# Weight sums of an encoder step, formed in DRAM: four 4 MB halves at once, or four groups of 512 columns spread over the program

## The chip, the cores and the metric

One Trainium2 chip, one NeuronCore, one execution of the whole program. The metric is the device time in microseconds (us). Kernel before: 3052.26 us, the median of three runs (3049.77 to 3056.08).

## The reference, cut to what matters

The program is one inference step of a hybrid encoder layer over 2048 prompt rows and 32 sample rows of width 1024. Three head groups (stick-breaking attention A, chunk-band softmax attention B, a gated recurrence C) work on one input projection; then come an output projection and a squared-ReLU MLP:

```
h = x + mixed @ w_o                          # 1024 x 1024
u = relu(rmsnorm(h, norm_ffn) @ w_up)        # 1024 x 4096
y = h + (u * u) @ w_down                     # 4096 x 1024
```

The product with `w_up` is done as a 2 x 2 block product with 7 multiplications in place of 8. Four of its seven weight factors are sums of the quadrants of `w_up`, each 512 rows x 2048 columns of float32, 4 MB. With w11 the top left quadrant, w21 the top right, w12 the bottom left and w22 the bottom right (the names of the changed code), they are:

```
sums[0] = w21 + w22      sums[1] = w11 + sums[0]
sums[2] = w11 + w21      sums[3] = w12 + sums[1]
```

They lie in `scratch_sums` in DRAM. GpSimd's DMA queue makes them: plain copies of a quadrant into its place, then DMAs that add another quadrant (or an earlier sum) to what lies there.

## The kernel before, in words

The program has three stages, one after the other: `front` (to about 329 us of the profile), `middle` (to about 1426 us) and `merge_and_ffn`, the last.

**The middle** runs four pieces of work as generators, interleaved by `plan`, a list of 846 letters. Each engine goes through that list on its own: at each letter it issues what the named piece has for that turn. B (96 turns, plan steps 0 to 168) is the chunk-band attention, A (196 turns, steps 160 to 572) the stick-breaking attention, C (169 turns, steps 565 to 845) the recurrence, and D (385 turns) a dense projection whose matmuls lie between the turns of the others. A DMA placed "at step k" on GpSimd is issued when GpSimd's own stream gets there, so it can run ahead of the other engines wherever GpSimd has nothing to wait for. SyncE (SP) issues every other DMA of the program, in one order: loads of keys, values and queries (L920 to L935), reloads of x (L564), stores of projected columns (L572, L577), loads of the recurrence (L1369 to L1389).

The sums are made by GpSimd beside that work. `begin_sums` at step 8 issues the four 4 MB copies (L1769); `add_halves` at step 282 waits for them and issues two adding DMAs (L1774); `add_third` at step 423 (L1778) and `add_fourth` at step 564 (L1782) issue one each, each after a wait for what it adds to. GpSimd waits for the last at the end of the middle. Its other work there: the mask of attention A (L976), scaling of a gated output (L590), the mask table (L1738 to L1759) and parts of C.

**The last stage** runs over three thirds of the rows (6 + 6 + 5 tiles of 128 rows and one of 32), `t` = 0, 1, 2. A third begins with the output projection, tile by tile (L2643); in it GpSimd turns each tile's sum of squares into a scale (L2140, L2143), 17 times in the whole stage. Then come 16 steps `p` of 256 hidden columns. `up(t, p, z)` (L2682) does the seven products z; `down(t, p)` (L2715) multiplies by `w_down` and adds into six accumulators through VectorE (L2481). The chunks of z = 6, 7, 5 and 3 come from `scratch_sums`, columns 128p to 128p + 127; those of 1, 2 and 4 from `w_up`. Each is 256 KB in 512 rows of 512 bytes, loaded by SP (L2028) into one of four staging buffers `stu`, rounded by ScalarE into one of seven buffers `uw..h` (L2166), the rest formed by VectorE in `uw..l` (L2350). VectorE's `uw..l` frees the staging buffer, and SP's next load waits for it. A step also loads 1 MB of `w_down` (L2038, one buffer `std`; split at L2180 and L2356). SP issues all this in one order; a load that waits holds back all behind it.

Of the kernel before, what the change touches and what calls it, by code (L numbers as in the profile page):

```python
# [15 lines left out]
ALU = mybir.AluOpType  # L16
# [1612 lines left out]
def middle(nc, ring, w_o, xhi, xlo, xt, w_in, lower_bounds, onorm, proj, tr, sources_a, sources_b, bias, sources_c, states, mix,  # L1629
           w_up, sums, used):  # L1630
# [4 lines left out]
    with ctx:  # L1635
# [16 lines left out]
        sum_begun, sum_added = S.sem("md_sum_begun"), S.sem("md_sum_added")  # L1652
# [83 lines left out]
        def _(pool):  # L1736
# [28 lines left out]
            copied, added = half_sums(w_up, sums)  # L1765

            def begin_sums():
                for out, half in copied:
                    nc.gpsimd.dma_start(out, half).then_inc(sum_begun, 16)  # L1769

            def add_halves():
                pool.wait_ge(sum_begun, 64)
                for out, half in added[0:2]:
                    nc.gpsimd.dma_start(out, half, accum_op=ALU.add, max_dma_last_dim=8192).then_inc(sum_added, 16)  # L1774

            def add_third():
                pool.wait_ge(sum_added, 32)
                nc.gpsimd.dma_start(added[2][0], added[2][1], accum_op=ALU.add, max_dma_last_dim=8192).then_inc(sum_added, 16)  # L1778

            def add_fourth():  # L1780
                pool.wait_ge(sum_added, 48)
                nc.gpsimd.dma_start(added[3][0], added[3][1], accum_op=ALU.add, max_dma_last_dim=8192).then_inc(sum_added, 16)  # L1782

            beside = {masks_at: make_masks, 8: begin_sums}
            for k, do in enumerate((add_halves, add_third, add_fourth)):
                beside[len(plan) * (2 + k) // 6] = do
            run(Dn.gpsimd(pool), B.gpsimd(pool), A.gpsimd(pool), C.gpsimd(pool), beside)
            pool.wait_ge(sum_added, 64)
# [17 lines left out]
def half_sums(w_up, sums):  # L1806


    half, rows = DFF // 2, D // 2
    top, low = slice(0, rows), slice(rows, D)  # L1810
    one, two = slice(0, half), slice(half, DFF)
    first = [(sums[0], w_up[top, two]), (sums[1], w_up[top, one]), (sums[2], w_up[top, one]), (sums[3], w_up[low, one])]
    added = [(sums[0], w_up[low, two]), (sums[2], w_up[top, two]), (sums[1], sums[0]), (sums[3], sums[1])]
    return first, added


def merge_and_ffn(nc, raw_at, nat_at, wo, nat2, mix, x, w_o, norm_ffn, w_up, w_down, sums, y):
# [16 lines left out]
    with ctx:  # L1834
# [297 lines left out]
        def _(pool):  # L2132
# [5 lines left out]
            for n, r in enumerate(r for th in FT for _, r in th):  # L2138
                pool.wait_ge(s["squared"], n + 1)
                nc.gpsimd.tensor_scalar(rstd[0:r, n:n + 1], ss[0:r, n:n + 1], 1.0 / D, EPS,  # L2140
                                        ALU.mult, ALU.add).then_inc(s["mean_ready"], 1)
                pool.wait_ge(s["mean_ready"], n + 1)
                nc.gpsimd.tensor_tensor(rstd[0:r, n:n + 1], rstd[0:r, n:n + 1], mhalf[0:r, 0:1],  # L2143
                                        ALU.pow).then_inc(s["rstd_ready"], 1)
# [599 lines left out]
def build(nc, a, outs):  # L2744
# [35 lines left out]
    kept = Map(nc, nc.sbuf_base, "")  # L2780
    with ExitStack() as ctx:
# [11 lines left out]
               (a["state_c"][0, 0], [csp[0, 0], css[0, 0]]), mix, a["w_up"][0], sums, used)  # L2793
# [26 lines left out]
```

## Time and profile before

| | |
|---|---|
| Runs (median of three) | 3052.26 us |
| The profiled execution | 3049.58 us |
| Its span, first to last instruction | 3047.8 us |
| TensorE matmul busy | 94% of the span |
| VectorE, ScalarE, GpSimd busy | 61%, 39%, 11% |
| TensorE's mean granted clock | 0.977 of 2.4 GHz |
| GpSimd's DMA queue | 33.55 MB, 8 DMAs of 4 MB |

The profile is of one execution, all times in us from its span's start. "Idle" of an engine is time in which it ran no instruction; the releaser named after it is what ended the last wait. The granted clock has two levels here, 2.4 GHz (1.0) and 1.2 GHz (0.5). DMA share is the mean busy share of the 16 DMA engines; q0 is GpSimd's DMA queue, q1 that of SP. A DMA's time "to landing" runs from its issue to its completion.

### The profile page before, as it was taken

How to read it: one execution, taken by the hardware profiler on the slowest of the kernel's cores; microseconds unless marked ns; L12 is line 12 of the kernel's file. 1: busy time of each engine (PE TensorE's matmuls, PEld its weight loads, DVE VectorE, ACT ScalarE, POOL GpSimd, SP SyncE). 2: the span in 40 equal slices, each digit the busy share in tenths (PEclk: the TensorE clock that was granted, in tenths of full speed). 3: DMA queues.
4: the chain of work that ended last, by engine and by line, in shares of the span. 5: the costliest groups of instructions: out<-in, count | busy, mean ns of one | idle time of the engine just before them, and what ended most of it. 6: DMA issues, size and time to landing. Idle time of an engine off the chain costs nothing.

```text
span 3047.8 us, 46651 instructions
## 1 busy us (share of the span) xinstructions
PE 2858.7 (94%) x17560; PEld 2502.4 (82%) x17560; DVE 1861.4 (61%) x2988; ACT 1182.1 (39%) x2448; POOL 336.9 (11%) x512
## 2 busy tenths in 40 slices
PE   7999589996998979987999999999999999999998
PEld 5788478885887879976888898988898988788887
DVE  5554244464655646786576666657666666587776
ACT  3331156543554523323343343334343433254442
POOL 2222110011000114563000000000000000000000
PEclk9999799998998989999999999999999999999999
DMA  8733642249333374452133232252332322444342
GB/s 263 250 126 121 235 144 80 80 127 232 95 101 97 94 204 136 133 184 100 60 116 92 83 104 87 91 193 72 91 104 87 104 86 96 151 118 135 114 128 96
DMA packets 412433, 381.90 MB, mean 125 GB/s; under 512 B 58124, under 2 KB 361838, under 8 KB 408114
## 3 DMA queue, kind: packets, MB, share of 16 engines
q1 hardware_dynamic: 407986, 345.37, 36.4%
q0 software_dynamic: 4224, 33.55, 4.3%
q8 instruction: 141, 2.31, 0.3%
q14 instruction: 82, 0.67, 0.1%
HBM read 310.81 MB, written 101.33 MB: 135 GB/s over the span
## 4 chain that ended last, share of the span: by engine, by line
PE 48%; DVE 2%; ACT 1%; issue 1%; DMA 1%; POOL 0%; POOLq 0%; DVEq 0%; ACTq 0%; SPq 0%
PE mf_psO L2715 23%; PE mf_psT L2682 18%; PE mf_psO L2643 5%; PE mf_psT L2617 1%; PE mf_psO L2682 1%; PE mf_psO L2701 0%; DMA mf_stu<-scratch_sums 0%; DVE mf_acc L2481 0%; DVE mf_hs L2432 0%; DVE mf_acc L2420 0%; DVE mf_dwl L2356 0%; ACT mf_psO L2222 0%; DMA mf_std<-in_w_down 0%; DVE mf_ow L2343 0%; DVE mf_uw2l L2350 0%
## 5 line engine op out<-in xcount | busy, mean ns | idle before, releaser
L2715 PE MATMUL mf_psO<-mf_dwh,mf_u 128*128 128x512 f32 x1920 | 613.2, 396 | 3.1 <-DVE mf_acc L2481 2.5
L2481 DVE TENSOR_TENSOR mf_acc<-mf_psO,mf_acc 128x1024 f32<-128x1024 f32 x256 | 313.2, 1223 | 279.7 <-PE mf_psO L2715 279.7
L2715 PEld LDWEIGHTS mf_psO<-mf_dwh,mf_u 128*128 128x128 f32 x1920 | 360.0, 188 | 101.6 <-issue 13.2
L2715 PE MATMUL mf_psO<-mf_dwl,mf_u 128*128 128x512 f32 x960 | 379.2, 395 | 0.0
L2180 ACT ACTIVATE mf_dwh<-mf_std 128x512 fp32r<-128x512 f32 x180 | 103.1, 624 | 518.3 <-PE mf_psO L2715 513.6
L2715 PEld LDWEIGHTS mf_psO<-mf_dwl,mf_u 128*128 128x128 f32 x960 | 180.0, 188 | 41.6
L994 ACT ACTIVATE md_wT<-md_psW 128x512 f32<-128x512 f32 (+4 forms) x232 | 128.5, 554 | 195.5 <-PE md_psW L1251 195.1
L438 PE MATMUL pj_psO<-pj_whi,xhi 128*128 128x512 f32 (+1 forms) x408 | 164.0, 402 | 0.4 <-DVE pj_wlo L359 0.4
L1070 DVE TENSOR_TENSOR_SCAN md_cp<-md_Aub,md_cp 128x512 f32<-128x512 f32 (+1 forms) x100 | 130.3, 1309 | 55.1 <-ACT md_Aub L1008 54.5
L438 PE MATMUL pj_psO<-pj_wlo,xhi 128*128 128x512 f32 (+1 forms) x408 | 162.4, 398 | 0.0
L438 PE MATMUL pj_psO<-pj_whi,xlo 128*128 128x512 f32 (+1 forms) x408 | 162.2, 398 | 0.0
L698 PE MATMUL md_psD<-wlo,xhi 128*128 128x256 f32 (+1 forms) x544 | 159.2, 293 | 0.0
L698 PE MATMUL md_psD<-whi,xlo 128*128 128x256 f32 (+1 forms) x544 | 159.0, 292 | 0.0
L698 PE MATMUL md_psD<-whi,xhi 128*128 128x256 f32 (+1 forms) x544 | 158.7, 292 | 0.0
L695 PE MATMUL md_psD<-xhi,whi 128*128 128x384 f32 (+1 forms) x384 | 136.8, 356 | 8.9 <-DVE wlo L636 8.9
L2140 POOL TENSOR_SCALAR mf_rstd<-mf_ss 128x1 f32<-128x1 f32 (+1 forms) x17 | 5.2, 305 | 1221.5 <-ACT mf_psO L2222 1221.5
L1175 PE MATMUL md_psZ<-md_KT,md_qhi 128*128 128x512 f32 (+5 forms) x288 | 99.9, 347 | 35.8 <-ACT md_Aub L1008 28.1
L2356 DVE TENSOR_TENSOR mf_dwl<-mf_std,mf_dwh 128x512 fp32r<-128x512 f32 x180 | 115.7, 685 | 20.7 <-ACT mf_dwh L2180 19.9
L695 PE MATMUL md_psD<-xlo,whi 128*128 128x384 f32 (+1 forms) x384 | 127.2, 331 | 0.0
L695 PE MATMUL md_psD<-xhi,wlo 128*128 128x384 f32 (+1 forms) x384 | 126.9, 331 | 0.0
L2457 DVE TENSOR_TENSOR mf_hs<-mf_hs 128x384 f32<-128x384 f32 (+1 forms) x186 | 95.6, 514 | 28.9 <-ACT mf_hs L2245 28.6
L2245 ACT ACTIVATE mf_hs<-mf_hs 128x384 f32<-128x384 f32 (+1 forms) x138 | 68.2, 494 | 111.3 <-DVE mf_hs L2449 85.9
(344 smaller groups left out, 7241.3 us busy)
## 6 DMA issues: line engine op xcount, KB each, us to landing
mf_std<-in_w_down SPq DMA_DIRECT2D x48, 1024.0 KB, 5.2
mf_stu<-scratch_sums SPq DMA_DIRECT2D x192, 256.0 KB, 2.9
mf_stu<-in_w_up SPq DMA_DIRECT2D x144, 256.0 KB, 3.6
wst<-in_w_in SPq DMA_DIRECT2D x24, 1024.0 KB, 5.3
scratch_sums<-in_w_up POOLq DMA_DIRECT2D x6, 4096.0 KB, 39.1
pj_wst<-in_w_in SPq DMA_DIRECT2D x36, 512.0 KB, 5.9
scratch_proj<-pj_ob SPq DMA_DIRECT2D x48, 256.0 KB, 2.0
pj_xin<-in_x_prompt SPq DMA_DIRECT2D x16, 512.0 KB, 7.3
```

Of the source, the lines that this page charges most:

```text
L438: last = nc.tensor.matmul(psO[n % NO][0:r, :], xa[:, k, c], wa[m % 2][:, k, :], start=k == 0 and j == 0, stop=k == KD - 1 and j == 2)
L695: last = nc.tensor.matmul(psD[n % NB][:, 0:r], wa[q % 2][:, k, e * P:(e + 1) * P], xa[:, k, cols], start=m == 0, stop=m == 23)
L698: last = nc.tensor.matmul(psD[n % NB][0:r, 0:256], xa[:, k, cols], wa[q % 2][:, k, :], start=m == 0, stop=m == 23)
L994: last = nc.scalar.activation(wT[j % 4][:, 0:full, 0:r], psW[j % WB][:, 0:full, 0:r], ACT.Copy)
L1070: nc.vector.tensor_tensor_scan(out=cp[i % NW][0:r, 0:w][:, ::-1], data0=u[0:r, 0:w][:, ::-1], data1=u[0:r, 0:w][:, ::-1], initial=init_v, ...
L1175: last = nc.tensor.matmul(psZ[i % ZB][0:r, x0:x1], qq[q][:, h, 0:r], KT[:, h, c0 + x0:c0 + x1], start=first, stop=not first)
L2180: nc.scalar.activation(d_buf(p)[0][:, cols], std[:, cols], ACT.Copy).then_inc(s["whi_d"], 1)
L2356: nc.vector.tensor_tensor(lo[:, cols], std[:, cols], hi[:, cols].bitcast(F32), ALU.subtract).then_inc(s["wlo_d"], 1)
L2481: nc.vector.tensor_tensor(acc[0:r, pos, :], psO[k % 2][0:r, :], acc[0:r, pos, :], ALU.add).then_inc(s["o_out"], 1)
L2643: last = nc.tensor.matmul(psO[k % 2][0:r, cols], xs[xa], ow[q][wa][:, w0:w0 + 512], start=at == 0 and j == 0 and e == 0, stop=at == 3 and ...
L2682: last = nc.tensor.matmul(out, wa[:, kk, :], xa[:, kk, 0:HB[t]], start=not again and kk == 0 and q == 0, stop=kk == KH - 1 and q == 2, ski ...
L2715: last = nc.tensor.matmul(psO[k % 2][0:r, cols], u[:, f, ua, c:c + P], wa[:, w0:w0 + 512], start=j == 0 and q == 0, stop=j == 1 and q == 2)
```

## The change

The eight DMAs of 4 MB become 32 of 1 MB: each half is cut into four groups of 512 columns. A group is eight DMAs: four copies, the first and second add after all four copies, the third add after those two, the fourth after the third. Rows of a DMA are now 2048 bytes long instead of 8192; each DMA still has 512 rows.

- Group 0 is made in the middle, one DMA at each of steps 200, 240, 280 and 320 (copies) and 370, 420, 470 and 520 (adds).
- Groups 1, 2 and 3 are made in the last stage by GpSimd, straight after the scales of the first third's six tiles: four copies in a row, then the adds with their waits, then the next group.
- SP waits, before each load of a chunk from `scratch_sums` in the first third, until the group that holds its columns is complete: p = 0 to 3 lie in group 0, 4 to 7 in group 1, 8 to 11 in group 2, 12 to 15 in group 3.
- GpSimd's wait at the end of the middle for the last add goes away.

```diff
-            beside = {masks_at: make_masks, 8: begin_sums}
-            for k, do in enumerate((add_halves, add_third, add_fourth)):
-                beside[len(plan) * (2 + k) // 6] = do
+            steps = {200: lambda: halves.copy(0, 0), 240: lambda: halves.copy(0, 1), 280: lambda: halves.copy(0, 2),
+                     320: lambda: halves.copy(0, 3), 370: lambda: halves.add_first(pool, 0),
+                     420: lambda: halves.add_second(pool, 0), 470: lambda: halves.add_third(pool, 0),
+                     520: lambda: halves.add_fourth(pool, 0)}
+            beside = {masks_at: make_masks, **steps}
             run(Dn.gpsimd(pool), B.gpsimd(pool), A.gpsimd(pool), C.gpsimd(pool), beside)
-            pool.wait_ge(sum_added, 64)
...
+class HalfSums:
+    GROUPS = 4
...
+        self.cols = DFF // 2 // self.GROUPS
...
+    def copy(self, g, i):
+        half = (self.w21, self.w11, self.w11, self.w12)[i]
+        self.nc.gpsimd.dma_start(self.of(self.sums[i], g), self.of(half, g)).then_inc(self.begun, 16)
+
+    def add(self, g, i, half):
+        self.nc.gpsimd.dma_start(self.of(self.sums[i], g), self.of(half, g), accum_op=ALU.add, max_dma_last_dim=8192
+                                 ).then_inc(self.added, 16)
+
+    def add_first(self, pool, g):
+        pool.wait_ge(self.begun, 64 * (g + 1))
+        self.add(g, 0, self.w22)
+
+    def add_second(self, pool, g):
+        pool.wait_ge(self.begun, 64 * (g + 1))
+        self.add(g, 2, self.w21)
+
+    def add_third(self, pool, g):
+        pool.wait_ge(self.added, 64 * g + 32)
+        self.add(g, 1, self.sums[0])
+
+    def add_fourth(self, pool, g):
+        pool.wait_ge(self.added, 64 * g + 48)
+        self.add(g, 3, self.sums[1])
...
@@ load_u, on SP
+                p, z = up_order[pos]
+                if t == 0 and z in (5, 6, 7, 3):
+                    sp.wait_ge(halves.added, 64 * (p * P // halves.cols + 1))
                 sp.dma_start(stu[:, c % NST, :].rearrange("p (k n) -> p k n", k=KH), chunk_src(*up_order[pos])
...
@@ GpSimd in the last stage, after the scales of third t
+                if t == 0:
+                    for g in range(1, halves.GROUPS):
+                        for i in range(4):
+                            halves.copy(g, i)
+                        halves.add_first(pool, g)
+                        halves.add_second(pool, g)
+                        halves.add_third(pool, g)
+                        halves.add_fourth(pool, g)
```

## Rows read from the trace of the kernel before

**Rows 1.** The page: busy tenths of TensorE in 40 equal slices, and its DMA share
```profile
PE   7999589996998979987999999999999999999998
DMA  8733642249333374452133232252332322444342
```

**Rows 2.** TensorE's waits from 326 to 1420 us: total, times, longest
```profile
PE md_psT L1200 <- DVE md_khl L1094: 45.6, 4, 25.0
PE md_psZ L1175 <- ACT md_Aub L1008: 28.1, 1, 28.1
PE md_psZ L1578 <- DMA md_rcg<-scratch_proj: 17.1, 1, 17.1
...
PE md_psZ L1187 <- DVE md_bt L1053: 8.2, 1, 8.2
```

**Rows 3.** DMA issues by line, whole program: count, KB each, median us to landing
```profile
mf_stu<-scratch_sums SPq DMA_DIRECT2D x192, 256.0 KB, 2.9
...
md_rcg<-scratch_proj SPq DMA_DIRECT2D x16, 256.0 KB, 5.2
```

**Rows 4.** Stretches with sums under way: each engine's busy us, PEclk, DMA share, GB/s
```profile
335.00:390.00 55.00, 18.93 (x90) 15.90 (x89) 7.35 (x14) 5.22 (x10) 0.00 (x0) 0.72 1.00 335
712.00:757.00 45.00, 19.44 (x171) 17.03 (x169) 11.98 (x16) 7.52 (x16) 4.59 (x7) 0.76 1.04 224
900.00:924.00 24.00, 10.30 (x78) 9.19 (x74) 4.57 (x6) 4.84 (x9) 0.65 (x1) 0.76 1.02 215
1093.00:1115.00 22.00, 9.61 (x86) 9.10 (x86) 3.35 (x6) 3.83 (x8) 0.99 (x2) 0.82 1.05 221
```

**Rows 5.** DMA queues, 376 to 385 us (copies under way): packets, MB, engines' share
```profile
q0 software_dynamic: 350, 2.77, 92.6%
q1 hardware_dynamic: 350, 0.12, 5.2%
```

**Rows 6.** DMA queues, 715 to 750 us (two adds under way)
```profile
q0 software_dynamic: 878, 7.06, 96.9%
q1 hardware_dynamic: 832, 0.43, 6.1%
```

**Rows 7.** SP's issues, 695 to 800 and 1099 to 1113 us: start, duration
```profile
714.41 38.81 SPq L577 DMA_DIRECT2D scratch_proj<-md_ob  x1
...
1100.61 4.93 SPq L577 DMA_DIRECT2D scratch_proj<-md_ob  x1
1105.70 5.00 SPq L1388 DMA_DIRECT2D md_rcv<-scratch_proj  x1
1110.75 2.60 SPq L1389 DMA_DIRECT2D md_rcg<-scratch_proj  x1
```

**Rows 8.** Half-clock stretches 346:370, 383.5:397, 735:766, 912.6:929.7, 1107:1124, their sum
```profile
sum 102.60, PE 27.02 PEld 23.52 DVE 14.47 ACT 7.54 POOL 7.05; mean PE 5.40 PEld 4.70 DVE 2.89 ACT 1.51 POOL 1.41
```

**Rows 9.** GpSimd in order of time, near 402 and near 1512 us
```profile
402.49 0.58 POOL L953 TENSOR_SCALAR_AFFINE_SELECT md_negm<-md_negm 128x1 f32<-128x1 f32 x2
...
1511.77 0.55 POOL L2143 TENSOR_TENSOR mf_rstd<-mf_rstd,mf_mhalf 128x1 f32<-128x1 f32 x1
```

**Rows 10.** DMA queues, 1636 to 1667 us (one step p)
```profile
q1 hardware_dynamic: 3968, 2.88, 31.8%
```

**Rows 11.** SP and ScalarE in order of time, last stage, chunk loads and splits
```profile
1581.11 3.17 SPq L2028 DMA_DIRECT2D mf_stu<-scratch_sums  x2
...
1598.46 0.36 SPq L2028 DMA_DIRECT2D mf_stu<-scratch_sums  x1
...
1548.15 0.63 ACT L2166 ACTIVATE mf_uw4h<-mf_stu 128x512 fp32r<-128x512 f32 x1 [2.22 <-DMA mf_stu<-scratch_sums]
...
1605.97 0.62 ACT L2166 ACTIVATE mf_uw4h<-mf_stu 128x512 fp32r<-128x512 f32 x1
```

**Rows 12.** The chain that ended last: two pieces, one step p
```profile
1604.98 16.80 PE mf_psO L2715 x72
1621.78 14.56 PE mf_psT L2682 x84
```

More of the change, by code:

```diff
@@ L1629, in middle @@
 def middle(nc, ring, w_o, xhi, xlo, xt, w_in, lower_bounds, onorm, proj, tr, sources_a, sources_b, bias, sources_c, states, mix,
-           w_up, sums, used):
+           halves, used):
     ctx = ExitStack()
@@ L1651, in middle @@
         maskstep = S.sem("md_maskstep")
-        sum_begun, sum_added = S.sem("md_sum_begun"), S.sem("md_sum_added")
         Dn = dense(nc, sems, mp, ring, xhi, xlo, xt, w_in, lower_bounds, onorm, psD, proj, tr)
@@ L1763, in make_masks @@
                 assert step == MASKSTEPS
[L1765 to L1782, printed above, removed]
-            beside = {masks_at: make_masks, 8: begin_sums}
-            for k, do in enumerate((add_halves, add_third, add_fourth)):
-                beside[len(plan) * (2 + k) // 6] = do
+            steps = {200: lambda: halves.copy(0, 0), 240: lambda: halves.copy(0, 1), 280: lambda: halves.copy(0, 2),
[3 more added lines that the diff above has]
+            beside = {masks_at: make_masks, **steps}
             run(Dn.gpsimd(pool), B.gpsimd(pool), A.gpsimd(pool), C.gpsimd(pool), beside)
-            pool.wait_ge(sum_added, 64)
         @block.scalar
@@ L1803, in middle, with __init__, of, merge_and_ffn @@
     return nat_at, wo, nat
[L1806 to L1817, printed above, removed]
+class HalfSums:
+    GROUPS = 4
+    def __init__(self, nc, w_up, sums, begun, added):
+        self.nc, self.begun, self.added = nc, begun, added
+        self.cols = DFF // 2 // self.GROUPS
+        half, rows = DFF // 2, D // 2
+        top, low = w_up[0:rows, :], w_up[rows:D, :]
+        self.w11, self.w21 = top[:, 0:half], top[:, half:DFF]
+        self.w12, self.w22 = low[:, 0:half], low[:, half:DFF]
+        self.sums = sums
+    def of(self, w, g):
+        return w[:, g * self.cols:(g + 1) * self.cols]
+    def copy(self, g, i):
[16 more added lines that the diff above has]
+        self.add(g, 3, self.sums[1])
+def merge_and_ffn(nc, raw_at, nat_at, wo, nat2, mix, x, w_o, norm_ffn, w_up, w_down, sums, halves, y):
     NP = DFF // (2 * P)
@@ L2137, in _ @@
                                     base=0, pattern=[[-1, P]], channel_multiplier=1).then_inc(s["init"], 1)
[L2138 to L2144, printed above, removed]
+            n = 0
+            for t in range(NTH):
+                for _, r in FT[t]:
+                    pool.wait_ge(s["squared"], n + 1)
+                    nc.gpsimd.tensor_scalar(rstd[0:r, n:n + 1], ss[0:r, n:n + 1], 1.0 / D, EPS,
+                                            ALU.mult, ALU.add).then_inc(s["mean_ready"], 1)
+                    pool.wait_ge(s["mean_ready"], n + 1)
+                    nc.gpsimd.tensor_tensor(rstd[0:r, n:n + 1], rstd[0:r, n:n + 1], mhalf[0:r, 0:1],
+                                            ALU.pow).then_inc(s["rstd_ready"], 1)
+                    n += 1
+                if t == 0:
[6 more added lines that the diff above has]
+                        halves.add_fourth(pool, g)
         @block.scalar
@@ L2780, in build @@
     kept = Map(nc, nc.sbuf_base, "")
+    halves = HalfSums(nc, a["w_up"][0], sums, nc.alloc_semaphore("sum_begun"), nc.alloc_semaphore("sum_added"))
     with ExitStack() as ctx:
@@ L2792, in build @@
                (lambda t0, r: proj[IC, t0:t0 + r, :], lambda t0, r: proj[GC, t0:t0 + r, :]),
-               (a["state_c"][0, 0], [csp[0, 0], css[0, 0]]), mix, a["w_up"][0], sums, used)
-    merge_and_ffn(nc, kept.base, nat_at, wo, nat, mix, x, a["w_o"][0], a["norm_ffn"][0], a["w_up"][0], a["w_down"][0], sums, y)
+               (a["state_c"][0, 0], [csp[0, 0], css[0, 0]]), mix, halves, used)
+    merge_and_ffn(nc, kept.base, nat_at, wo, nat, mix, x, a["w_o"][0], a["norm_ffn"][0], a["w_up"][0], a["w_down"][0], sums, halves, y)
 _INS = ["x_prompt", "x_sample", "cache_a_k", "cache_a_v", "cache_b_k", "cache_b_v", "state_c", "norm_mix", "w_in",
```

## Prediction

> **What bounds the kernel now.** I read the page's slices first: TensorE is at nine tenths nearly everywhere, and the lowest slices of the middle (5 at 305 to 381 us, 6 at 686 to 762) lie where the DMA row is high (6 and 9) [rows 1]. Then TensorE's waits in the middle [rows 2]: four kinds hold 99 us. By their time they are 25.0, 2.8 and 8.2 us between 341 and 389, 28.1 from 731, 14.5 from 910 and 17.1 from 1103 (the row of 45.6 holds 25.0, 2.8, 14.5 and one of 3.3 at 595, near no sum). That is 95.7 us.
>
> Next the stretches in which the eight 4 MB DMAs run: all DMA engines are busy (share 1.00 to 1.05) while TensorE works 18.9 of 55, 19.4 of 45, 10.3 of 24 and 9.6 of 22 us [rows 4]. The queue counts say why. With copies under way q0 and q1 each finish 350 packets, with adds 878 and 832 [rows 5, 6]: the DMA engines take one packet of each queue in turn. One of q0 is 8 KB and takes 0.926 x 9 us x 16 / 350 = 0.38 us (copy) or 0.969 x 35 x 16 / 878 = 0.62 us (add). Those of SP are small, so SP gets 5% or 6% of the time, and its small stores and loads pile up: an issue is stuck 38.8 us, others 4.9 and 5.0 [rows 7]. So at four places TensorE is bound by SP's starved queue, and everywhere else in the middle by its own work. In the last stage it is the chain without a gap, 16.80 + 14.56 = 31.36 us a step [rows 12].
>
> **1. The bursts leave the middle: -101 us.** The waits of 95.7 us go, but for what would stand there anyway. At 341 the loads that were waited for stand in SP's queue behind the four bias loads (4 x 128 x 640 floats, 1.3 MB), about 4 us at the rate of this stretch (335 GB/s [rows 4]): I leave 3. At 1103 the load waited for was issued at 1110.75 after two stuck issues of 4.93 and 5.00 us [rows 7]; without those it is issued near 1101.5, and 5.2 us of landing [rows 3] leave 5 of the 17.1. So 95.7 - 8 = 88 us. The idle engine also falls to half clock at these places: in five stretches of 102.6 us it is busy 27.0 us at 0.50 [rows 8], which at full clock is 13.5. Sum 101. Bounds: 80 (a fifth of the stalls turns out to be latency of the attention stages) and 109 (nothing remains). The reason against a smaller number is that every one of the four long waits starts 7 to 19 us after the burst does, and ends with it.
>
> **2. Group 0 in the middle: +1 us.** Eight DMAs of 1 MB. Step 200 comes before the first masked unit of A, so GpSimd passes it as soon as it is through A's opening (402.49 [rows 9]): the first copy runs in B, not in A. The others lie over A, the adds about 70 us apart. A copy puts 32 packets on each DMA engine. A packet of 2048 bytes is not in the trace; in proportion to size it is 0.38 / 4 = 0.095 us (copy) and 0.62 / 4 = 0.155 (add), and it can't be more than 0.38 and 0.62. I take the proportional value, since the packets' time is that of their bytes at the fabric's rate: 2.77 MB of copies in 8.3 us is 332 GB/s. So an add holds SP's queue for 32 x 0.155 = 5.0 us, a copy 3.0. The third add, a burst of 24 us, stalled TensorE for 14.5 [rows 2, 4]: 9.5 us of a burst are covered by loads made ahead. 5.0 is less. Bounds 0 and 4 x 3.0 + 4 x 5.0 = 32, all uncovered. GpSimd's own issues and waits are hidden: each DMA it waits for was issued 50 steps, some 70 us, before. What is queued behind such a wait are A's masks, which the chain needs; they are late only if an add takes over 60 us.
>
> **3. Groups 1 to 3 beside the last stage: +10 us.** They begin when GpSimd has done the sixth scale, 1511.77 + 0.55 [rows 9]. Engine time of a group: 128 packets x 0.095 + 128 x 0.155 = 32 us on each DMA engine; three make 96 us. SP's queue wants 31.8% of 31 us, 9.9 us a step, in 3968 / 16 = 248 packets of 0.040 us [rows 10]. A group then takes about 32 / (1 - 0.32) + three hand-overs of 2 to 3 us between add and add = 55 us, three 165, to about 1677. In a step's 31.4 us some 22 are free, so on the whole there is room; what costs is lateness of single loads.
>
> A chunk load is 32 packets on each engine. Beside adds it takes 32 x (0.155 + 0.040) = 6.2 us where it took 1.3: 5 us later, and a second and third behind it more, until the pair of adds is through (64 packets, 12.5 us). Beside copies it is 3 us later. Who has that much room? In a regular step the load issued at 1598.46 is used by ScalarE at 1605.97, and it lands in 2.9 us: 4.6 us of room [rows 3, 11]; VectorE comes to the result a little later still, which I put at 3 us more. At the start of the third there is none: ScalarE stands idle 2.22 us for the load that it uses at 1548.15 [rows 11]. VectorE takes these splits between its adds into the accumulators, which free TensorE's two output buffers, so a late chunk stops `down` as well. I take 2 us for the loads of 1526 to 1536 and 6 for those of 1545 to 1556, where the first and third adds of group 1 fall, and 0.5 for each of the four steps that follow: 8 + 2 = 10. Bounds: 0, and 3 x 16 = 48 (each group's adds, 4 x 5 us less 4 of room, in full).
>
> SP's new waits: for p = 0 to 3 they are met long before. The first one that could hold is that of p = 4, whose first summed chunk SP loads at 1581.11 [rows 11]. Group 1 is complete near 1512.3 + 55 = 1567, 14 us before; group 2 near 1622 for a wait at 1707, group 3 near 1677 for 1832. Cost 0; each us over 68 for group 1 would stop SP, and behind it the loads of `w_down` too. GpSimd's scales for the second third are due near 2080, long after. The wait removed at the end of the middle had been met since about 1115: 0.
>
> **Sum.** -101 + 1 + 10 = -90, against the profiled execution's 3049.6: 2959.6. The median of the runs stands 2.7 above that execution, so 2962.
>
> **Rivals.** *The late groups cost more (chance 0.18).* If packets of 2 KB are dearer than a quarter, or the queue's turn is longer, SP waits longer per packet. The rows show one packet for one, at 8 KB.
> The Trainium skill (DMA: Bandwidth & Descriptors, SWDGE vs HWDGE vs iDMA) says that an engine changes queue only at packet borders and that GpSimd's packets may hold several descriptors, preferably up to 4096 bytes. By that rule two rows of 2 KB could go in one turn, where the 8 KB rows of before could not show it; the trace agrees with the change of queue at each packet, and is silent on the pairing.
> Worked out from rows, two add packets in a turn make a chunk load 32 x (0.31 + 0.04) = 11.2 us, 10 later than now instead of 5; the 4.6 + 3 us of room are then passed in regular steps too, by 3 to 6 us in each of five steps, and the start costs 15 to 20: 35 to 50 in all. Time 2952 + 45 = 2997.
>
> *The stalls are only partly the bursts' (0.11).* TensorE then meets VectorE's or ScalarE's limits where it used to wait. For it: VectorE works 12.0 us of the 19.4 that TensorE works beside two adds, so it is not idle where TensorE runs [rows 4]. Against it: the slices between the bursts are at nine tenths [rows 1]. The lower bound above and 10 more: gain 60, time 2992.
>
> *The other side: a packet costs the same whatever its size (0.05).* The place is SP's wait at p = 4. With 0.38 and 0.62 us for 2 KB, a group takes 128 x 0.42 + 128 x 0.66 + 8 = 146 us. SP stops for 146 - 68 = 78 us, and at p = 8 and 12 until the third group is there: 3 x 146 - 320 = 118 us in all, more than the 101 gained. With 10 for contention: 3052 - 101 + 118 + 10 = 3079. It decides from 137 us a group (3 x 137 - 320 = 91). *That the change doesn't do what it says* holds for the first copy alone and costs nothing.
>
> **How the numbers follow.** Forecast 2962, chance 0.62, own range 2948 to 2978 (gain 109 less 5 to gain 80 less 6). The first two rivals reach to 3005, where the bounds 80 and 48 + 8 leave a gain of 24 at worst: the range 2946 to 3008 leaves out the third rival and the tails. A measurement of this kernel tells 0.2%, 6 us, from no change: faster 0.93 (forecast, two rivals, small rests), same 0.02, slower 0.05.
>
> **What would show it.** Steps 1 and 2: no wait of TensorE over 6 us from 341 to 1420 and full clock throughout; the last stage begins near 1326. If SP still has issues of over 5 us there, step 2 is wrong. Step 3: between about 1412 and 1577 (the old 1512 to 1677) ScalarE's split L2166 waits for DMAs, and the steps p there are longer than 31.36 by 10 us in all; the last add of group 1 lands before SP's first load of p = 4. A wait of TensorE or SP in which `scratch_sums` is the releaser, over 15 us long, makes step 3 wrong; a q0 packet far from 0.095 and 0.155 us says by which rival.

## The result and the profile after

The kernel after takes 2979.99 us (median of 4 runs, 2976.53 to 2983.62) against 3053.11 for the kernel before on the same chip: ratio 0.9761, 95% interval 0.9744 to 0.9778. The forecast was 2962 with a range of 2946 to 3008. The gain is 73 us where 90 were expected. The profiled execution of after took 2983.62 us (span 2981.9), 66 less than that of before. In the experiments below one execution of e7 (4061 us) and one of the kernel before (4044 us) were a third slower than all others, and the ratios leave both out.

The page of after, busy tenths of TensorE and DMA share, to be read beside [rows 1]:

```profile
PE   7999899899999999879889999999999999999998
DMA  7833332355334643522995232343223223343442
```

The low TensorE slices of the middle (the 5 and the 6) are gone. The DMA row has its 9 9 now from 1416 to 1565 us, in the last stage, where TensorE's row has two 8s that the kernel before does not have at the same work. TensorE's waits from 326 to 1320 us, beside [rows 2]:

```profile
PE md_psD L695 <- DVE wlo L636: 8.9, 1, 8.9
...
PE md_psT L1200 <- DVE md_khl L1094: 6.6, 3, 3.5
PE md_psZ L1175 <- DVE md_qlo L1117: 5.5, 1, 5.5
```

Neither the 25.0, 28.1, 14.5 and 17.1 us nor anything over 9 us is left. The first row is the start of the middle, which before has too (8.9). As a mark of the last stage's beginning I take ScalarE's third split of `w_o` in it (L2182 of after, L2156 of before; the first is 5.5 us earlier in both): it starts at 1335.9 us, where before has it at 1431.9, so 96 us earlier, at a forecast of 100. From that mark to the ScalarE instruction just before its first split of `w_o` for the second third (the same one in both traces) before takes 568.9 and after 599.7: 30.8 longer, at a forecast of 10. The rest of the stage is equal (1047.0 and 1046.4). So nearly the whole difference between forecast and result lies in the last stage's first third. Two windows of 166 us that begin with the same work there, before first, then after (columns as in [rows 4]):

```profile
1501.00:1667.00 166.00, 163.64 (x835) 147.91 (x834) 115.27 (x171) 71.60 (x137) 0.74 (x2) 1.00 0.35 105
```

```profile
1405.00:1571.00 166.00, 143.38 (x682) 127.69 (x681) 95.89 (x143) 60.76 (x115) 19.79 (x25) 0.93 0.94 227
```

The DMA share goes from 0.35 to 0.94, TensorE does 682 matmuls in place of 835 and stands idle for 20 us more, and its mean granted clock is 0.93. Its waits from 1405 to 1620 us in after:

```profile
PE mf_psO L2741 <- DVE mf_acc L2507: 11.8, 4, 5.0
PE mf_psT L2708 <- ACT mf_hs L2260: 6.0, 1, 6.0
PE mf_psO L2708 <- DVE mf_uw6l L2376: 2.3, 1, 2.3
```

ScalarE's waits in the same stretch name what is behind VectorE and ScalarE:

```profile
ACT mf_uw4h L2192 <- DMA mf_stu<-scratch_sums: 17.6, 3, 10.2
ACT mf_uw6h L2192 <- DMA mf_stu<-scratch_sums: 10.4, 3, 5.4
```

and so do the pieces of the chain that ended last:

```profile
1433.78 11.04 DMA mf_stu<-scratch_sums
...
1453.16 10.68 DMA mf_stu<-scratch_sums
...
1468.71 22.92 DMA mf_stu<-scratch_sums
...
1523.83 24.17 DMA mf_stu<-scratch_sums
```

A chunk load that landed in 2.9 us [rows 3] takes 11 to 24 us there. Which of GpSimd's DMAs run beside them can be read from its timeline below. The load of 1433.78 runs beside the first two adds of group 1, that of 1453.16 beside the third. The two longest, 22.9 and 24.2 us, run beside the last add of a group and the four copies of the next, which follow it without a pause; three or four chunk loads stand in SP's queue there, one behind the other. TensorE's waits go the same way: 2.3 and 5.0 us beside group 1's adds, then 6.0 at 1487 and 3.1 and 3.0 near 1545, both at such a run of add and copies.

Group 1's own copies cost nothing. In after's queues from 1416 to 1430 us there are 974 packets of q0 and none of SP. SP issues no load from 1413.1 to 1430.0, and in e3, which has no late groups, it pauses at the same place (1412.7 to 1429.6). The next two loads land in 4.6 and 4.7 us.

The four stretches of half clock in this third (1447.2:1450.6, 1464.2:1471.0, 1491.5:1498.3, 1549.6:1556.4), their sum:

```profile
sum 23.80, PE 19.31 PEld 16.73 DVE 13.49 ACT 7.71 POOL 7.63; mean PE 4.83 PEld 4.18 DVE 3.37 ACT 1.93 POOL 1.91
```

Each begins in a wait of TensorE or within 2 us of its end. TensorE is busy for 19.3 us at 0.50 there, of which 9.7 are lost. With the 20.1 us of the three rows of waits that is 29.8 of the 30.8.

What the packets cost, after, 1540 to 1544 us (copies under way), then 1432 to 1450 (the first two adds of group 1):

```profile
q0 software_dynamic: 354, 1.37, 89.7%
q1 hardware_dynamic: 354, 0.17, 15.5%
```

```profile
q0 software_dynamic: 1056, 2.10, 70.2%
q1 hardware_dynamic: 2834, 1.41, 31.0%
```

The queues still change at every packet where both have work (354 to 354; in the second window SP also has the time for itself before the adds' first packets and after their last). But a copy's packet holds 1.37 MB / 354 = 3.9 KB, two rows of 2 KB, and takes 0.897 x 4 x 16 / 354 = 0.16 us; an add's packet holds 2.10 MB / 1056 = 2 KB, one row, and takes 0.702 x 18 x 16 / 1056 = 0.19 us.
The Trainium skill (DMA: Bandwidth & Descriptors, SWDGE vs HWDGE vs iDMA) prefers packets of up to 4096 bytes that may hold several descriptors. The copies here agree with it (two rows, 3.9 KB); the adds keep to one row of 2 KB, and the 8 KB rows of the kernel before went as one packet each [rows 5].

GpSimd's timeline of after, group 1 (start, duration, in brackets the idle time before and what ended it):

```profile
1416.24 2.62 POOL L1806 DMA_DIRECT2D scratch_sums<-in_w_up  x4
1432.80 2.12 POOL L1809 DMA_DIRECT2D scratch_sums<-in_w_up  x2 [13.94 <-DMA scratch_sums<-in_w_up]
1450.31 1.01 POOL L1809 DMA_DIRECT2D scratch_sums<-scratch_sums  x1 [15.39 <-DMA scratch_sums<-in_w_up]
1463.76 1.00 POOL L1809 DMA_DIRECT2D scratch_sums<-scratch_sums  x1 [12.44 <-DMA scratch_sums<-scratch_sums]
1464.39 2.92 POOL L1806 DMA_DIRECT2D scratch_sums<-in_w_up  x4
```

From the first copy to the last add's landing (1478.4) it is 62 us, at a forecast of 55, and q0 has hardly a pause: group 2's four copies are issued beside group 1's last add.

### The profile page after: what moved, and what is told of

It is laid out like the page before. It is cut to its first block, busy times and chain, and to the rows that moved or that the text cites. A ratio compares the mean times of both kernels' runs of the same rounds, so it can differ in the third digit from the quotient of the medians.

```text
span 2981.9 us, 46738 instructions
## 1 busy us (share of the span) xinstructions
PE 2862.9 (96%) x17560; PEld 2504.2 (84%) x17560; DVE 1862.2 (62%) x2988; ACT 1183.0 (40%) x2448; POOL 357.6 (12%) x536
## 4 chain that ended last, share of the span: by engine, by line
PE 48%; DMA 3%; DVE 3%; ACT 1%; issue 1%; POOL 0%; POOLq 0%; DVEq 0%; ACTq 0%; SPq 0%
PE mf_psO L2741 22%; PE mf_psT L2708 18%; PE mf_psO L2669 5%; DMA mf_stu<-scratch_sums 3%; PE mf_psT L2643 1%; PE mf_psO L2708 1%; PE mf_psO L2727 0%; DVE mf_acc L2507 0%; DVE mf_hs L2458 0%; DVE mf_acc L2446 0%; DVE mf_dwl L2382 0%; ACT mf_psO L2248 0%; DMA mf_std<-in_w_down 0%; DVE mf_uw2l L2376 0%; DVE mf_ow L2369 0%
## 5 line engine op out<-in xcount | busy, mean ns | idle before, releaser
L2741 PE MATMUL mf_psO<-mf_dwh,mf_u 128*128 128x512 f32 x1920 | 618.6, 399 | 14.8 <-DVE mf_acc L2507 14.2
L2382 DVE TENSOR_TENSOR mf_dwl<-mf_std,mf_dwh 128x512 fp32r<-128x512 f32 x180 | 115.7, 686 | 20.8 <-ACT mf_dwh L2206 20.1
L348 ACT ACTIVATE pj_sq<-pj_psO 128x512 f32<-128x512 f32 (+1 forms) x51 | 30.4, 597 | 207.6 <-PE pj_psO L438 207.4
```

The lines of the kernel that those rows point to most:

```text
L2382: nc.vector.tensor_tensor(lo[:, cols], std[:, cols], hi[:, cols].bitcast(F32), ALU.subtract).then_inc(s["wlo_d"], 1)
L2741: last = nc.tensor.matmul(psO[k % 2][0:r, cols], u[:, f, ua, c:c + P], wa[:, w0:w0 + 512], start=j == 0 and q == 0, stop=j == 1 and q == 2)
```

## The experiments

Each ratio is against runs of the kernel before on the same chip. Three chips were used (e1 to e4; e5, e6, e8, e9; the rest), and the kernel before has a median of 3056.2 us on each. e4, e3 and e5 leave sums out and so give the output of other weights: they are there for their time alone. "Third begins" and "first third" are the two marks of the section above, both from one profiled execution. The six kernels whose middle is the same as after's (after, e3, e5, e6, e8, e12) begin the third at 1331.0 to 1337.7, which is how far single executions differ. The last two thirds, beside which no kernel makes sums, take 1046.4 to 1054.2 us, and the first third of e2, with no sums beside it either, is 4.3 us longer than before's: a difference of 4 us in the last column says nothing.

| | median us | ratio (95%) | third begins | first third |
|---|---|---|---|---|
| before (profiled execution) | 3056.2 | 1 | 1431.9 | 568.9 |
| after | 2980.0 | 0.9761 (0.9744 to 0.9778) | 1335.9 | 599.7 |
| e4 no sums | 2949.9 | 0.9651 (0.9633 to 0.9669) | 1326.4 | 569.1 |
| e3 no late groups | 2955.7 | 0.9672 (0.9655 to 0.9689) | 1335.4 | 569.0 |
| e1 all 32, one every 20 steps | 2982.6 | 0.9759 (0.9734 to 0.9785) | 1365.1 | 568.9 |
| e2 all 32, one every 11 steps | 2987.1 | 0.9771 (0.9748 to 0.9794) | 1362.7 | 573.2 |
| e5 late copies alone | 2969.5 | 0.9715 (0.9691 to 0.9739) | 1331.0 | 583.8 |
| e6 late adds in 512 B packets | 2963.5 | 0.9694 (0.967 to 0.9718) | 1337.7 | 580.3 |
| e8 groups 2 and 3 paced | 2970.2 | 0.9717 (0.9696 to 0.9739) | 1334.0 | 584.6 |
| e9 spread from the front stage on | 2962.9 | 0.9695 (0.9672 to 0.9717) | 1337.7 | 569.4 |
| e7 before, bursts cut into 2 KB rows | 3052.9 | 0.9989 (0.9977 to 1.0002) | 1431.9 | 568.9 |
| e11 before, adds in 1 KB packets | 3047.4 | 0.9965 (0.9951 to 0.9978) | 1422.3 | 568.7 |
| e10 e9 with adds in 512 B | 2960.2 | 0.9677 (0.9655 to 0.9698) | 1334.7 | 573.2 |
| e12 e8 with late adds in 512 B | 2959.8 | 0.9681 (0.9665 to 0.9697) | 1336.0 | 573.8 |

### What each step is worth: e4 and e3

```diff
 e4: the steps, GpSimd's late groups and SP's waits on halves.added are gone, and
-  5: sums[0], 6: sums[1], 7: sums[2], 3: sums[3]
+  5: w_up[half[0], f:2 * f], 6: w_up[half[1], 0:f], 7: w_up[half[1], f:2 * f], 3: w_up[half[0], 0:f]
 e3: the loop over g in range(1, GROUPS) is gone, and for z in (5, 6, 7, 3)
+  p = p % 4
```

> No weight sums at all: the 32 DMAs and their waits are left out, and the chunks that came from scratch_sums are read from quadrants of w_up, so the output is that of other weights. Floor for both kernels. Queue theory (SP's queue gets one packet for each of GpSimd's, and only bursts longer than the loads made ahead cost anything): the middle is as in the changed kernel, 96 us shorter than before or up to 5 more, and the last stage's first third is 31 us shorter than in the changed kernel: 3053 - 96 - 3 = 2945 to 2954. Rival, bytes theory (each MB of sums costs the same wherever it runs, 33.5 MB cost 96 + what group 0 still costs): group 0's 8.4 MB cost a further 30 us in the middle, so 2915 to 2925.

> The changed kernel without groups 1 to 3 (left out; the chunks of p = 4 to 15 read group 0's columns instead, so most of the sums are wrong). Queue theory: all of the 31 us by which the first third grew come back, 2980 - 31 = 2949, and it is within 5 us of the kernel without any sums, since single DMAs of 1 MB are covered by loads made ahead. Bytes theory: 25 to 30 us above the kernel without sums. A third theory, that the first third grew for SP's new waits or for another order of the loads, would leave part of the 31 in: over 2960.

Without any sums the ratio is 0.9651, with group 0 alone 0.9672, with all four 0.9761. Times 3056, the three steps are -106.7 us, +6.4 and +27.2, together -73. The forecast had -101, +1 and +10. Both expectations fell on the side of the queue theory (2945 to 2954 for e4); e3 is 6 us above e4 where at most 5 were expected, and the intervals of the two overlap. By the profiles, from 326 us to the beginning of the third, e4 has 92.4 us less idle time of TensorE than before (54.3 against 146.7) and 13.1 us less busy time for the same matmuls, which is the half clock. TensorE's waits of e4 from 326 to 1320 us:

```profile
PE md_psD L695 <- DVE wlo L636: 8.9, 1, 8.9
...
PE md_psZ L1175 <- DVE md_qlo L1117: 5.4, 1, 5.4
...
PE md_psT L1200 <- DVE md_khl L1094: 3.5, 2, 3.2
```

So the 5.5 us of `md_qlo` in after belong to the attention's own start, and group 0 in the middle costs about 3 us of `md_khl` in after (2.6 of them beside its first add) and 5 in e3's profile (8.9 in all). In e3 the first third is 569.0 us, as before: a window of the same work as the two above has

```profile
1404.00:1570.00 166.00, 163.33 (x834) 147.53 (x833) 115.06 (x170) 71.50 (x137) 0.85 (x3) 1.00 0.35 105
```

All of the 31 us, the half clock too, come from the late groups.

### Does a spaced DMA cost nothing anywhere in the middle: e1 and e2

```diff
-  steps = {200: lambda: halves.copy(0, 0), ..., 520: lambda: halves.add_fourth(pool, 0)}
+  at = 206 + 20 * (8 * g + i)      # e2: 206 + 11 * (8 * g + i); none is late
```

> All four groups in the middle, one 1 MB DMA every 20 steps of the plan from step 206 (over attention A and the recurrence C), none in the last stage. Queue theory: each DMA is 6 to 13 us long, as those of group 0, and covered; 2949 plus 1 us of GpSimd issue for each DMA that falls into C, where GpSimd is on the chain: 2950 to 2965. Bytes theory: 24 more DMAs cost as much as they did in the last stage, 31 us: 2980.

> The same with one DMA every 11 steps from step 206, so that all 32 fall into attention A and none into C. They then follow each other after some 15 us where an add takes 10 to 13 us, so SP's queue shares the DMA engines two thirds of the time. Queue theory: loads made ahead cover 9.5 us of one burst and are made up for in the pause after it; 2950 to 2960, and no worse than one every 20 steps. If the pauses are too short, waits on DMAs of A's keys and queries appear in TensorE's waits and the time is 2965 or more. Bytes theory: 2980.

Both missed the queue theory's range and landed at the 2980 of the bytes theory: moving all 32 into the middle frees the first third (568.9 in e1) and gives as much back before it: the third begins 30 us later than in e3. It is not one price per MB. TensorE's waits of e1 from 326 to 1320 us:

```profile
PE md_psZ L1578 <- DVE md_rcqp L1511: 10.8, 13, 2.7
PE md_psT L1200 <- DVE md_khl L1094: 10.4, 3, 6.4
PE md_psT L1200 <- DVE md_o L1146: 10.1, 3, 5.2
...
PE md_psZ L1578 <- DMA md_rcg<-scratch_proj: 3.3, 1, 3.3
```

The gaps lie at 619 to 671 us and at 720 and 763, then there are none of over 1.9 us up to 1041, though eleven DMAs run there, and from 1041 a few of 1.7 to 3.3 us in the recurrence (e4 has one of 2.5 there). Up to the third e1 has 17.7 us more idle time of TensorE than after and 11.5 us more busy time at the lower clock. At the start of A the eight DMAs of 589 to 768 us, one every 14 to 33 us, are not all covered; after's copies at 624, 666 and 714, one every 45 us, caused no wait over 1.6 us there. e2, with one DMA every 8 to 20 us, has waits of 3.9, 5.0 and 11.5 us between 618 and 700. In the second half of A DMAs every 17 to 32 us are covered. So the start of A covers less; how much of it is the spacing and how much the exact place of a DMA is not shown.

### Which part of the late groups costs: e5, e6, e8, e12

```diff
 e5:  no adds for g = 1 to 3 (SP loads group 0's columns), copies as they are
 e6:
-  accum_op=ALU.add, max_dma_last_dim=8192
+  accum_op=ALU.add, max_dma_last_dim=512 if g else 8192
 e8:
+  if g > 1:
+      pool.wait_ge(s["up_done"], 21 + 3 * (8 * (g - 2) + i))      # ahead of each of a group's eight DMAs
 e12: e8 and e6 together
```

> The changed kernel with only the four copies of groups 1 to 3 in the last stage, none of their adds (left out; the chunks of p = 4 to 15 read group 0's columns, so most sums are wrong). In the changed kernel a copy's packets turned out to be 4096 bytes and 159 ns, 256 a DMA, an add's 2048 bytes and 176 ns, 512 a DMA. Queue theory: SP loses 16 x 159 ns = 2.5 us to a copy and 32 x 176 ns = 5.6 us to an add, so 12 copies in three bursts of 10 us cost little, 2 to 8 of the late groups' 27 us: 2958 to 2964. Bytes theory: half of the bytes moved, half of the cost, 13 us: 2969.

> The changed kernel with the adds of groups 1 to 3 cut into packets of 512 bytes in place of 2048. Queue theory: SP's queue gets one packet after every small one, so a chunk load beside an add is late by 32 x some 50 ns = 1.6 us and not 5.6; the late groups then cost 8 to 15 us in place of 27 and the time is 2960 to 2970, if the longer adds (four times the packets) do not hold up a group. Bytes theory: the same bytes, 2980 or slower, since small packets carry more overhead.

> The changed kernel with groups 2 and 3 paced: GpSimd issues each of their DMAs only after three more chunks of the up product are done, so one DMA every 13 us or so in place of four copies at once and adds back to back; group 1 as it was. Queue theory: a single DMA is covered by the 4.6 us of room of a regular step, so groups 2 and 3 cost 0 to 4 us in place of 27 x 2/3 = 18 (or less, if the tight start of the third holds most of it), 2962 to 2972. Bytes theory: 2980, since nothing is taken away.

> After the change with both remedies of the late groups: groups 2 and 3 issued one DMA per three chunks of the up projection, and the late adds in packets of 512 bytes. Alone they gave 2970.2 (spacing) and 2963.5 (packets); with no late groups at all it is 2955.7. If the two work on different loads (the spacing on groups 2 and 3, the packets on all adds) they add up until the copies' share of group 1 is left: 2957 to 2962. If both only take away the same late loads of group 1: 2963 to 2970.

TensorE's waits in the first third, from 1405 us on: e5, e6, e8, e12 in this order, one fence each.

```profile
PE mf_psO L2739 <- DVE mf_acc L2505: 5.6, 1, 5.6
PE mf_psO L2706 <- DVE mf_uw6l L2374: 4.8, 1, 4.8
```

```profile
PE mf_psO L2742 <- DVE mf_acc L2508: 4.9, 2, 3.9
```

```profile
PE mf_psO L2740 <- DVE mf_acc L2506: 4.3, 2, 2.5
PE mf_psO L2707 <- DVE mf_uw6l L2375: 4.0, 1, 4.0
```

```profile
PE mf_psO L2741 <- DVE mf_acc L2507: 3.3, 1, 3.3
```

The first third is longer than e3's by 30.7 us (after), 14.8 (copies alone), 11.3 (small adds), 15.6 (paced) and 4.8 (both); by the ratios it is 27.2, 13.1, 6.7, 13.8 and 2.8. e6's profile is of its slowest execution (2974.0, the others near 2963.4), and e12 can't be told from e3. e6, e8 and e12 came out in the ranges of the queue theory. e5 did not: 2969.5 is the number of the bytes theory, against 2958 to 2964.

e5 does not show what the copies cost in after. With no adds between them the twelve copies follow each other from 1411 to 1464 us, so those of groups 2 and 3 fall on the tight loads that stand beside group 1's adds in after. And e6, which has after's twelve copies, four behind each group's last add, and the adds as well, loses less than e5. What e6 shows is that 20 of the 27 us go with the adds' packet size, and e8 that 13 to 15 go when groups 2 and 3 are spaced; how the 27 us divide into copies and adds is not shown. Small packets are slower to move the same bytes, and an add takes longer to land (13 to 24 us in e12), but SP waits less for its turn. Queues in e6, 1447 to 1458 us, one add of group 1 under way:

```profile
q0 software_dynamic: 1784, 0.91, 64.7%
q1 hardware_dynamic: 1782, 1.80, 60.0%
```

One for one again; 512 bytes cost q0 0.647 x 11 x 16 / 1784 = 0.064 us, and SP moves 1782 packets in 11 us, 162 a us, where its loads of a step want 3968 in 31 [rows 10], 128 a us. Pacing saves its 15 us with packets of 2 KB left as they are: group 1's adds are not paced and TensorE's waits beside them stay (4.0 and 2.5 us), but group 2's copies no longer run beside group 1's last add, and the waits of 6.0 and 6.1 us at such runs are gone but for one of 1.8 at 1621. e12, with both, is at 2959.8; that both together beat small packets alone (e6) is likely but not clear of noise, since the intervals overlap.

### Size of a packet or spacing: e7 and e11 on the kernel before

```diff
 e7: each of the eight DMAs, at its place, becomes four
-  nc.gpsimd.dma_start(out, half, ...).then_inc(...)
+  for g in range(4):
+      nc.gpsimd.dma_start(out[:, g * 512:(g + 1) * 512], half[:, g * 512:(g + 1) * 512], ...).then_inc(...)
 e11, at the adds only:
-  max_dma_last_dim=8192
+  max_dma_last_dim=1024
```

> The kernel before with each of its eight 4 MB DMAs issued as four of 1 MB, column group after column group, back to back at the same eight places; bytes, places and order are the same, only the rows of a packet are 2 KB instead of 8 KB (copies pair two rows, 4 KB). Theory A, the turn's length decides: SP's queue gets one packet for one of q0, so its turn comes after 0.16 to 0.18 us instead of 0.38 to 0.62. A load of 32 packets per engine then takes 32 x (0.18 + 0.04) = 7 us beside an add instead of 21. After the change three late groups, back to back and of such packets, cost 27 to 31 us, 10 a group; four groups here would cost 40 instead of the 100 that leaving the sums out gives back: 2990, range 2980 to 3005, and the long waits of TensorE near 341, 731 and 1103 shrink to 6 to 10 us each. Theory B, the bytes that stand in a burst decide, and only the spacing helped: the DMA engines are full for the same 32 MB, 3045 to 3060, waits as before.

> The kernel before with one number changed: the adds' rows are cut into packets of 1 KB instead of 8 KB; the four copies stay as they are, 8 KB. Measured packets of adds are 0.064 us for 512 bytes and 0.176 for 2048, so one of 1 KB is put at 0.105 (an estimate between the two). Theory A (turn's length): a load beside an add takes 32 x (0.105 + 0.04) = 5 us; the waits of TensorE at the three add places (28.1, 14.5 and 17.1 us, and some 8 of half clock) go but for a few us each, the one at the copies, 341 to 389, stays: 3053 less 50 to 65, that is 2988 to 3003, and TensorE's wait near 341 still over 20 us. Theory B (bytes in a burst): 3045 to 3060 with all waits where they were, or more, since a packet has a fixed part and the adds take longer in all.

e7 fell on the side of theory B, against what I believed: 0.9989, no difference. So did e11: 3047.4, where theory A had 2988 to 3003. Queues of e7 from 715 to 750 us, two adds' worth of 2 KB packets under way, beside [rows 6]:

```profile
q0 software_dynamic: 2818, 5.60, 88.7%
q1 hardware_dynamic: 2818, 1.54, 24.2%
```

SP's queue gets 2818 packets through where it got 832, 3.4 times as many, as theory A says. TensorE's waits from 336 to 1130 us say that it doesn't help enough:

```profile
PE md_psT L1200 <- DVE md_khl L1094: 27.1, 3, 14.9
PE md_psT L1200 <- DVE md_o L1146: 22.2, 4, 15.1
PE md_psZ L1578 <- POOL md_rcAt L1408: 20.6, 1, 20.6
PE md_psZ L1175 <- ACT md_Aub L1008: 11.9, 1, 11.9
PE md_psZ L1175 <- DVE md_qlo L1120: 10.6, 1, 10.6
```

A new stall is among them. GpSimd's timeline of e7, 1086 to 1118 us:

```profile
1086.99 3.11 POOL L1772 DMA_DIRECT2D scratch_sums<-scratch_sums  x3
1117.60 1.01 POOL L1772 DMA_DIRECT2D scratch_sums<-scratch_sums  x1 [27.50 <-issue]
1118.23 1.37 POOL L1408 MEMSET md_rcAt<- 128x512 f32 x2
```

The fourth DMA is issued only 0.5 us after the third has landed (1117.1), GpSimd stands 27.5 us with the recurrence's `md_rcAt` queued behind it, and that is the wait of 20.6. It takes the place of before's 17.1. The other waits, at the copies and the first three adds, are some 67 us against 78.6 in before [rows 2]. In all e7 has 7.2 us less idle time of TensorE than before up to the third (139.5 against 146.7), and 7.2 us more busy time: 59 of its busy us fall into half clock, 44 of before's. What e7 would have gained without the stop at the fourth DMA was not tried. e11 has the same trap at the pair of adds, where the second is issued 0.3 us after the first has landed (738.2):

```profile
708.78 3.94 POOL L1774 DMA_DIRECT2D scratch_sums<-in_w_up  x1 [0.19 <-issue]
738.43 3.86 POOL L1774 DMA_DIRECT2D scratch_sums<-in_w_up  x1 [25.70 <-issue]
```

TensorE waits 30.1 us there, and then 9.9. At the third and fourth adds one DMA stands alone and GpSimd is not stopped. TensorE's waits of e11 from 336 to 1130 us:

```profile
PE md_psT L1200 <- DVE md_o L1146: 42.0, 4, 30.1
PE md_psT L1200 <- DVE md_khl L1094: 30.2, 3, 25.1
...
PE md_psZ L1578 <- DMA md_rcg<-scratch_proj: 7.5, 1, 7.5
```

None is left at the third add (14.5 before), and 7.5 at the fourth (17.1 before), although each add takes 8 to 11 us longer to land. The third is no clean test of the size. The issue of this add takes 2.9 us (1.0 in before), its first packets come near 915 us, and SP's store of 912.70 has landed at 915.55, ahead of them; in before the same store, issued at 900.72, lands at 924.25, behind the add. From 916 to 932 us SP then moves 227 packets beside 2834 of q0. At the fourth add both queues are full: from 1102 to 1118 us each moves 2006 packets.

So neither theory is the whole. What fits is a rate: with both queues full SP gets one packet for one of q0, that is 832 / 35 = 24 a us beside 8 KB adds, 2818 / 35 = 81 beside 2 KB and 2006 / 16 = 125 beside 1 KB. What SP wants differs from place to place. e4, with no sums, moves 421 packets a us from 670 to 696 us, the work that before does beside its first two adds, 129 from 826 to 850 (the third) and 303 from 1001 to 1026 (the fourth). So the rate beside 1 KB nearly meets the want at the third add, and at no other. Falling behind for a short time is covered by loads made ahead: 9.5 us of before's third add were. A spaced copy of 1 MB is over in 6 to 9 us and a spaced add in 10 to 14; the first two adds of e7 last 57 us together, at 81 a us where 421 are wanted. The estimate (1 - rate / want) x length - 9.5 gives for before's first two adds (46 us) and its fourth (26 us) waits of 34 and 14 us, measured 28.1 and 17.1; for e7's first two (57 us) and third (37 us) 37 and 4, measured 32.0 and 9.0; for e11's fourth (37 us) 12, measured 7.5. It is off by 3 to 6 us everywhere, and half clock and a stopped GpSimd come on top.

### Spread wider: e9 and e10

```diff
 front: if n in [24, 26, ..., 46]: halves.next(pool)                  # 12 DMAs beside the input projection
 middle: steps 62, 74, ..., 158, each behind a wait for the dense unit done there; then 338, 358, ..., 538
 the order: all 16 copies first, then the adds; none is late.   e10: every add in 512 B packets
```

> All 32 DMAs of 1 MB in stretches where TensorE was never seen to wait: 12 in the second half of the first stage (one every two tiles), 9 in the band attention (paced by the dense projection's units), 11 in the second half of the stick-breaking attention, where the kernel with all DMAs in the middle had 11 of them and no gap over 1.5 us; all copies first, then the adds by group. Nothing beside the start of the stick-breaking attention, the recurrence or the last stage. Place theory (a DMA costs what its stretch has no loads made ahead for): 2950 to 2958, at most 8 above the kernel without sums, and faster than the changed kernel. Bytes theory: 2980, as with all of them in the middle.

> The version with 32 spread DMAs and none late (2962.9), with every add in packets of 512 bytes instead of 2048. Without any sums the kernel takes 2949.9, so 13 us are left. Theory A (turn's length): the adds' share of the 13 shrinks to a third, 2953 to 2959. Theory B (engine time decides once the DMAs are spread): packets of 512 bytes make the adds a third longer, 2963 to 2968.

e9 keeps out of the start of A and of the recurrence, and takes 2962.9: 17 us less than after, with one gap over 3 us that e4 hasn't, 4.4 at 747. It is 13 above e4, where at most 8 were expected, so a part of the place theory's forecast failed. Of the 18 us between the two profiled executions 6.6 lie in the last two thirds, beside which neither makes sums. In e10 (2960.2, between the ranges of its two theories) the smaller packets change nothing that can be told (0.9677 and 0.9695, the intervals overlap), and its profiled execution has 7.9 us of `md_khl` at 555 where others have 3 to 5. If the size of a packet still matters once the DMAs are spread, it is by less than these runs can tell. e9, e10 and e12 all beat both kernels; among themselves (2962.9, 2960.2, 2959.8) they can't be told apart.

## Why the prediction was right, and where it was off

The sign, the mechanism and the place hold: the four waits at the bursts went, the stage begins earlier by 96 us (forecast 100). The total is 18 us off, nearly all of it in step 3.

- **Step 1, the bursts leave the middle.** Forecast -101, shown by e4: -107. The terms were the waits (88) and the half clock (13); e4's profile has 92.4 us less idle and 13.1 us less busy time. One reading behind it was wrong: not every long wait ends with its burst, the first ends at 366.4 us and the last copy lands at 392.3. The rival that the stalls are only partly the bursts' is refuted: without the sums nothing over 9 us is left.
- **Its reason was too narrow.** I put the stall down to the turn of SP's queue, so that packets of a quarter would mean a quarter of the delay. e7 has the small packets in the old places and gains nothing, in part for a new stop of GpSimd; it is the length of an uninterrupted run of q0, together with the turn and with what SP wants at that place, that counts. What the change brought is the spacing. The sum was not touched by this, since it removed the bursts whole.
- **Step 2, group 0 in the middle.** Forecast +1 (0 to 32), e3 against e4: +6.4 in the ratios, with intervals that overlap. An add was put at 5.0 us; alone it lasts 10.1 to 13.4 in after, and the cover of 9.5 us was read at the third add, in the second half of A. Nevertheless four copies and four adds lost only 3 to 5 us in waits, 42 us and more apart; e1 and e2, whose DMAs stand closer, have waits of 2 to 11 us at the start of A. After's profile begins the third 9.5 us later than e4's, 4.1 idle and 5.5 busy: half clock again, of which two stretches (778 to 782 us and 1024 to 1027) are not in e4. Executions of the same middle differ by 7 us, so how much of this is group 0's is open.
- **Step 3, groups 1 to 3 late.** This is the term that was mis-sized: +10, shown by after against e3: +27.2, by the two profiles +30.7. Three things are in it. The half clock: I priced it in step 1 and forgot it here, 9.7 us. The waits: I allowed 8 us at group 1 and 2 for the steps that follow; they are 13.3 up to group 2's copies and 6.1 at group 3's. I placed them at the first and third adds (7.4 us came there), and called loads beside copies 3 us late; but the copies follow a group's last add without a pause, three or four loads queue up beside that run, and the loads of 22.9 and 24.2 us and the other 12.0 us of waits stand there. And the packets: I took 0.095 and 0.155 us for 2 KB, the copies come in pairs at 0.16, the adds at 0.18 to 0.19, so SP waits longer for each turn although the copies' bytes are no slower.
- **Its order of events** was right: SP has no wait on `scratch_sums`, group 1 is complete at 1478 (a group takes 62 us, forecast 55), 27 us before SP's first load that needs it (1505.2; forecast 14), and group 3 is complete at 1593, 376 us before GpSimd's first scale for the second third (1969.1).
- **The rival of dearer late groups** (2997, two add packets in a turn) named the right place with half of the right cause: the copies pair, the adds don't. That the result lies midway between it and the forecast is chance: the forgotten half clock alone makes 9.7 of the difference. The third rival, a packet that costs the same whatever its size, is refuted by 0.064 us for 512 bytes, 0.18 to 0.19 for 2 KB and 0.62 for 8 KB (adds).

That the profile would show full clock throughout from 341 us on was nearly so in the middle: pieces of 3.4 to 6.8 us remain near 560 and 584 us, which e4 has too, and near 778 and 1024, which it hasn't. The piece of 17 us at 1317, where the stage changes, stands at 1418 in before. One sum of the range does not fit either: the bounds 80 and 48 + 8 leave a gain of 24 us, which is 3028 and lies outside the 3008 given.

## What to carry to other kernels

A bulk transfer on another queue takes turns with the loads that the compute waits for. Price it by what the load queue still gets per us against what it wants at that place, times the length of the run without a pause, less the cover of the loads made ahead there; then add the half clock that comes with the waits of TensorE. Look for places where the load queue is silent anyway, as beside group 1's copies here. Spacing is the first remedy, a packet small enough that the load queue keeps up is the second, and the second needs care that the issuing engine isn't stopped by its own queue.

## What the runs showed of the hardware that I had not expected

- Plain copies with rows of 2 KB go out in 4 KB packets at 0.16 us, adds stay at one row a packet (0.18 to 0.19). An add costs twice a copy per byte: 0.63 and 0.31 us for 8 KB, medians of the packets' own records in the windows of [rows 6] and [rows 5]. (The 0.38 us of the prediction is a mean over the window.)
- GpSimd can be stopped at the issue of a DMA until all that it had issued has landed: 27.5 us at the last of four adds of 1 MB (e7), 25.7 at the second of two of 4 MB in 1 KB packets (e11). It isn't the number under way alone: earlier in e7 sixteen copies of 1 MB in a row, and later eight adds in a row, went out without a stop. What fills up, or wraps around, was not tried.
- Issuing an add takes longer with its packets: 1.0 to 1.5 us for 512 (after), 2.8 for 2048 (e12), 2.9 to 3.9 for 4096 (e11). It also grows with what stands before it: of e7's eight adds of 512 packets in a row the first takes 1.1 us and the last 3.9.
- A DMA that adds 1 MB takes 9.5 to 16.6 us to land (the median of after's sixteen is 13.1), though its packets take only 32 x 0.18 = 5.8 us of each DMA engine.
